# Token rows ahead of context rows in the third mixer, modulation rows kept in a 24-row table, and one PSUM bank per down-product unit in the last two MLPs

## The chip, the cores and the metric

One core of a Trainium2 chip runs the whole program: TensorE (PE), VectorE (DVE), ScalarE (ACT), GpSimd (POOL) and SyncE (SP), each with its own instruction queue. The metric is the device time of one execution in microseconds.

## What is computed

The reference is a chain of two blocks of two layers each on 256 tokens of 1024 columns, all in float32. The first block (two mixers, each followed by a mixture of 32 experts) is not touched by the change. The second block takes its result `x`, a context of 256 rows, and vectors `c`, `c_ctx`:

```
m_l = (silu(c) @ w_mod[i] + b_mod[i]);  m_c = (silu(c_ctx) @ w_mod[i] + b_mod[i])
sh1, sc1, g1, sh2, sc2, g2 = split(m_l, 6)          # csh1, csc1, ... of m_c
hl = modulate(x, norm1_g[i], sh1, sc1)              # rmsnorm * (1 + scale) + shift
i == 0: hc = modulate(ctx, norm1_g[i], csh1, csc1)
        ol = attention_mixer(hl, hc, ...)           # keys and values of ctx and tokens, queries of tokens
i == 1: ol = hyena_mixer(hl, ...)
x = x + g1 * ol
x = x + g2 * (square(relu(modulate(x, norm2_g[i], sh2, sc2) @ w1)) @ w2)
```

The attention mixer projects 1024 columns to a latent query (384 columns, `mla_cq`), a latent key and value (288, `mla_ckv`), 8 query heads (512, `gqa_q`) and 2 key and value heads (256, `gqa_kv`). Both latents are normed and projected again (`mla_q`, `mla_kv`). Eight heads of each kind attend, and `a_out` projects back.

## The kernel before

**Work and buffers.** Weights come in slabs of 128 x 4096 float32 (2 MB) through a ring of six places. SP issues all slab loads in one order, written out by hand (from line 776 on for the part that matters here), and each waits until the last reader of the slab six places back is done (`load`, line 682; `Plan.last_reader`). PSUM has eight banks of 128 x 512; `Plan.take` hands them out in turn, and each filling is a unit with two semaphores, full and drained. Every engine walks its own list of steps. A PE product waits in `claim` until its bank is drained. The plan (`make_plan`, lines 183 to 281), SP, POOL, PE, ACT and DVE all spell the same order.

**Modulation rows.** A row of `m_l` is wanted on all 128 partitions. In one way PE multiplies a slab of `w_mod` with `silu(c)` widened to 128 columns (`c_product`, line 958). In the other DVE forms a partial product over the eight k-tiles (`multiply_c`, line 2061: one tensor_scalar and seven scalar_tensor_tensor of 128 x 512), PE sums it over partitions with a matrix of ones (`sum_up`, line 963), and DVE adds the sum to a bias that POOL loaded as a broadcast row. `pre1` is shift and scale of the first norm (four slabs), `gate1` g1 (two), `pre2` shift and scale of the second norm (four), `gate2` g2 (two).

**Third mixer.** PE goes through the four `mod0.pre1` slabs: a product for the context and a sum for the tokens from each (from line 1303 on). DVE adds all eight to their biases, then norms and modulates first the context, then the tokens (lines 2552 to 2558; `norm_both`, `norm_tile` at line 1969), with ACT's square sums and roots in between (`tile_stats`, line 1537). PE transposes each (`turn`), waits for both, and projects tokens and context together (line 1316). DVE's norms of the latents and heads need a root from ACT; on ACT `root(384, 2)` and `root(256, 4)` stand behind the copies of all four projections (lines 1839, 1840), `root(64, 16)` and `root(64, 8)` behind the copies of the transposed latents. Then come `mla_q`, `mla_kv`, rotations on DVE, transposes of the heads (`mla_qT`, `mla_kT`, PE line 927), and two attentions of 16 steps. After `gqa_o` PE transposes the result (`turn.a_out`) and multiplies with `a_out`; DVE now makes six partial products (`gate1` two, `pre2` four), then runs `modulated_after` (line 2012): gate times result added to h, bias sums, norm.

**The last two MLPs.** Eight steps j of 512 hidden columns. ACT makes a rounded high part of each half slab (`make_high`), DVE the low part (`make_low`, line 2625), both four parts ahead; PE forms each float32 product from three (lines 1398 to 1400 for `w1`, 1411 to 1413 for `w2`). The `w2` half of a step fills four units (two tiles by two halves) in banks 4 to 7, each of 12 matmuls, and DVE adds each to `mlp_y` in SBUF (lines 2653, 2655). At the end `mlp_y` is multiplied by `gate2` and added to h (lines 2666, 2667). The order of one step's halves is MLP_PARTS:

```
MLP_PARTS = [(w, j - w, half) for j in range(MLP_STEPS + 1) for w in range(2) if 0 <= j - w < MLP_STEPS
             for half in range(2)]
```

## Time and profile before

| what | value |
|---|---|
| median of 3 runs | 2659.91 us (2653.01 to 2660.47) |
| profiled execution, its own time | 2655.35 us |
| its span, first to last instruction | 2653.6 us |
| mean granted TensorE clock | 0.939 |
| busy: PE, DVE, ACT | 2370.4, 1965.2, 1342.4 us |
| DMA | 607.80 MB, mean 229 GB/s |

Times in the rows are microseconds from the span's start. The third mixer runs from 1555.8 to about 1855, its MLP to 2047, the fourth mixer to about 2450, the last MLP to 2641. A row's first number is its start or stretch; an idle time in brackets names what ended it. The granted clock is 1.00 at 2.4 GHz and 0.50 at 1.2 GHz. A float32 product of 512 columns leaves two matmul records, a transpose one, an MLP product (rounded parts) one.

### The profile page before, as it was taken

How to read it: one execution, taken by the hardware profiler on the slowest of the kernel's cores; microseconds unless marked ns; L12 is line 12 of the kernel's file. 1: busy time of each engine (PE TensorE's matmuls, PEld its weight loads, DVE VectorE, ACT ScalarE, POOL GpSimd, SP SyncE). 2: the span in 40 equal slices, each digit the busy share in tenths (PEclk: the TensorE clock that was granted, in tenths of full speed). 3: DMA queues.
4: the chain of work that ended last, by engine and by line, in shares of the span. 5: the costliest groups of instructions: out<-in, count | busy, mean ns of one | idle time of the engine just before them, and what ended most of it. 6: DMA issues, size and time to landing. Idle time of an engine off the chain costs nothing.

```text
span 2653.6 us, 29973 instructions
## 1 busy us (share of the span) xinstructions
PE 2370.4 (89%) x11050; PEld 1740.7 (66%) x11050; DVE 1965.2 (74%) x2383; ACT 1342.4 (51%) x1477; POOL 23.9 (1%) x45
## 2 busy tenths in 40 slices
PE   7998999999989879999999987897998668876998
PEld 6557777777764557777777744563887226733887
DVE  3747999999983649999999972558776543468875
ACT  3236888888861428888888821351432011101432
POOL 0000000000000000000000000000000000000000
PEclk9998999999999989999999997898999688988999
DMA  8315989988883217988888872307375401307370
GB/s 323 125 66 202 374 356 373 370 359 359 358 325 104 96 63 317 379 363 361 363 362 362 358 273 81 127 1 258 139 281 183 180 32 64 127 8 272 130 272 16
DMA packets 116505, 607.80 MB, mean 229 GB/s; under 512 B 5300, under 2 KB 8428, under 8 KB 91644
## 3 DMA queue, kind: packets, MB, share of 16 engines
q1 hardware_dynamic: 111536, 588.83, 57.2%
q0 software_dynamic: 4880, 17.76, 1.8%
q8 instruction: 60, 0.98, 0.2%
q14 instruction: 29, 0.24, 0.0%
HBM read 605.51 MB, written 1.05 MB: 229 GB/s over the span
## 4 chain that ended last, share of the span: by engine, by line
PE 54%; DVE 23%; issue 13%; ACT 9%; DVEq 1%; DMA 0%; POOL 0%; SPq 0%; ACTq 0%
PE bank L902 10%; DVE slab_parts L2406 8%; ACT high L1706 5%; PE bank L914 4%; PE bank L1185 4%; PE bank L1137 3%; PE bank L1001 3%; PE bank L1164 2%; PE bank L1398 2%; PE bank L1400 2%; PE bank L1399 2%; PE bank L1126 2%; PE bank L1411 2%; PE bank L1413 2%; PE bank L1412 2%
## 5 line engine op out<-in xcount | busy, mean ns | idle before, releaser
L2406 DVE TENSOR_TENSOR slab_parts<-ring,high 128x2048 fp32r<-128x2048 f32 x384 | 862.3, 2288 | 38.9 <-ACT high L1706 34.4
L1706 ACT ACTIVATE high<-ring 128x2048 fp32r<-128x2048 f32 x384 | 728.5, 1914 | 43.9 <-PE bank L1137 35.6
L1137 PE MATMUL bank<-high,xT_parts 128*128 128x512 f32 x1024 | 294.5, 409 | 18.1 <-DVE slab_parts L2406 14.1
L1137 PE MATMUL bank<-slab_parts,xT_parts 128*128 128x512 f32 x1024 | 278.9, 394 | 0.0
L1549 ACT ACTIVATE arena<-bank 128x512 f32<-128x512 f32 (+4 forms) x162 | 89.4, 586 | 360.8 <-PE bank L902 99.4
L902 PE MATMUL bank<-ring,xT 128*128 128x512 f32 (+3 forms) x576 | 238.3, 575 | 10.2 <-DVE xT L2036 6.2
L1137 PEld LDWEIGHTS bank<-high,xT_parts 128*128 128x128 f32 x1024 | 184.5, 190 | 78.7 <-DVE slab_parts L2406 38.6
L1137 PEld LDWEIGHTS bank<-slab_parts,xT_parts 128*128 128x128 f32 x1024 | 193.9, 189 | 45.5
L1712 ACT ACTIVATE arena<-bank 64x512 f32<-64x512 f32 (+2 forms) x352 | 184.7, 534 | 61.6 <-PE bank L1164 51.5
L902 PEld LDWEIGHTS bank<-ring,xT 128*128 128x128 f32 x576 | 111.3, 194 | 133.9 <-issue 123.3
L1569 ACT ACTIVATE high<-ring 128x2048 fp32r<-128x2048 f32 x64 | 121.8, 1912 | 87.5 <-PE bank L1413 82.2
L2625 DVE TENSOR_TENSOR slab_parts<-ring,high 128x2048 fp32r<-128x2048 f32 x64 | 146.2, 2292 | 20.5 <-ACT high L1569 20.2
L1398 PE MATMUL bank<-xT_parts,high 128*128 128x256 f32 x512 | 148.1, 289 | 10.2 <-DVE slab_parts L2625 10.2
L1164 PE MATMUL bank<-high,hidden_parts 128*128 128x512 f32 x512 | 150.1, 415 | 7.4 <-DVE hidden_parts L2428 4.7
L1400 PE MATMUL bank<-xT_parts,slab_parts 128*128 128x256 f32 x512 | 145.7, 285 | 0.0
L1399 PE MATMUL bank<-xT_low,high 128*128 128x256 f32 x512 | 145.6, 284 | 0.0
L1164 PE MATMUL bank<-slab_parts,hidden_parts 128*128 128x512 f32 x512 | 141.1, 397 | 0.0
L1154 PEld LDWEIGHTS bank<-arena 128*128 128x128 f32 x1024 | 121.8, 192 | 5.9 <-ACT arena L1712 3.1
L1154 PE MATMUL bank<-arena 128*128 128x64 f32 x1024 | 123.0, 273 | 2.2 <-ACT arena L1712 2.2
L887 PE MATMUL bank<-resident,arena 128*128 128x128 f32 x208 | 43.6, 385 | 84.1 <-DVE arena L1981 39.2
L1185 PE MATMUL bank<-arena 128*128 128x512 f32 x256 | 115.3, 592 | 2.7 <-DVE arena L2436 2.7
L1542 ACT ACTIVATE arena<-h 128x1024 f32<-128x1024 f32 x18 | 18.9, 1052 | 192.7 <-DVE stat L1966 192.6
(360 smaller groups left out, 3739.1 us busy)
## 6 DMA issues: line engine op xcount, KB each, us to landing
ring<-in_moe_w_gate SPq DMA_DIRECT2D x64, 2048.0 KB, 8.6
ring<-in_moe_w_up SPq DMA_DIRECT2D x64, 2048.0 KB, 9.1
ring<-in_moe_w_down SPq DMA_DIRECT2D x64, 2048.0 KB, 9.4
ring<-in_mlp_w SPq DMA_DIRECT2D x32, 2048.0 KB, 13.3
ring<-in_w_mod SPq DMA_DIRECT2D x24, 2048.0 KB, 8.0
ring<-in_even_w_in SPq DMA_DIRECT2D x7, 2048.0 KB, 21.4
ring<-in_odd_w_in SPq DMA_DIRECT2D x6, 2048.0 KB, 10.6
ring<-in_h_w_in SPq DMA_DIRECT2D x6, 2048.0 KB, 8.5
```

Of the source, the lines that this page charges most:

```text
L902: last = mm(banks[u.bank][:, 0:n], lhs(k, tile), w[:, k, c0:c0 + n], start=(k == 0), stop=(k == k_tiles - 1))
L1137: last = mm(dst[:, :], seated2[:, 4 * half + k, e], part_[:, k, :], start=(half == a == k == 0), stop=(half == a == 1 and k == 3))
L1154: last = mm(dst[:, (4 * w + f) * SEATS:(4 * w + f + 1) * SEATS], raw[:, w, f * P:(f + 1) * P], fold, start=True, stop=True)
L1164: last = mm(dst[:, :], hidden2[:, f], part_[:, f, :], start=(a == f == 0), stop=(a == 1 and f == 3))
L1185: ins = mm(banks[bank][:, :], weightedT[:, (j // 2) * P:(j // 2 + 1) * P], pair_y[:, (j % 2) * 512:(j % 2 + 1) * 512], start=first, stop=last)
L1398: mm(dst, w_high[:, k, fs], xT_high[:, k, :], start=(k == 0), stop=False)
L1399: mm(dst, w_high[:, k, fs], xT_low[:, k, :], start=False, stop=False)
L1400: last = mm(dst, w_low[:, k, fs], xT_high[:, k, :], start=False, stop=(k == KD - 1))
L1706: act_fn(hi, weight_half(layer, name, half), ACT.Copy).then_inc(sem(f"high{layer}"), 1)
L1712: act_fn(dst, src(banks[u.bank]), func).then_inc(done or moe_drained[layer][u.bank], 1)
L2406: v.tensor_tensor(low, w, hi.bitcast(F32), ALU.subtract).then_inc(sem(f"low{layer}"), 1)
L2625: v.tensor_tensor(w_low, loaded, w_high.bitcast(F32), ALU.subtract).then_inc(sem("mlp_low"), 1)
```

## The change

- **Order of tokens and context.** In `mod0.pre1` the sums of the tokens' last slab come ahead of the context's last product. All four tile_ready calls come at the start, so ACT does both square sums at once. The tokens are normed and transposed first, PE runs `mla_cq` (tokens only) and then transposes the context; statistics of the context get columns of their own.
- **Roots.** Each root stands on ACT right behind the copies of the projection that it norms.
- **Early modulation rows.** DVE makes the partial products of `gate1` and of the shift half of `pre2` before the attention, writing each over the first k-tile of its own slab. `collect` sums two of them on PE into two rows of a 24 x 512 unit (stationary operand: a column of ones among 24), and `keep` adds the unit to `mod_rows`, a 24 x 512 table of all biases, one DMA, in a part of `routers` that is free by then. After `gqa_o` four `spread` products copy one row each to 128 partitions, and ACT copies them to `gate` and `shift`. The scale half of `pre2` goes the old way. SP loads `gate1` ahead of `mla_q` and `pre2` ahead of `a_out`; POOL no longer loads two of the broadcast bias rows.
- **Down products.** Both MLPs keep the four units of the `w2` products open in banks 4 to 7 over all eight steps; DVE's adds and `mlp_y` go. The slabs of steps 0 to 6 are released by a new counter, `mlp_out_used`. In the last step PE waits for half 1's parts, then finishes both halves of tile 0, then of tile 1, and DVE multiplies by `gate2` straight out of PSUM.

The plan's `take` and slab calls follow the new order; the diff leaves them out, with the new columns of the statistics.

```diff
+def mlp_out_used(layer, j, half):
+
+    return 2 * (MLP_STEPS - 1) * layer + 2 * j + half + 1
+
...
+    def collect(self, name, slabs):
+
+        self.take(name)
+        for slab, i in slabs:
+            self.last_reader[self.slabs[slab][i]] = self.units[name][-1]
...
-            if j > 0:
-                self.take(name + ".out", 4, (4, 5, 6, 7))
+            if j == MLP_STEPS:
+                self.take(name + ".out", 4, OUT_BANKS)
                 self.slab(name + ".w2", self.units[name + ".out"][-1])
+            elif j > 0:
+                self.slab(name + ".w2", ("mlp_out_used", mlp_out_used(int(name[-1]), j - 1, 1)))
...
+        def mlp_part_used(eng, layer, n):
 
             w, j, half = MLP_PARTS[n]
-            return U[f"mlp{layer}.hidden"][2 * j + half] if w == 0 else U[f"mlp{layer}.out"][4 * j + 2 * half + 1]
+            if w == 0:
+                full(eng, U[f"mlp{layer}.hidden"][2 * j + half])
+            elif j < MLP_STEPS - 1:
+                eng.wait_ge(sem("mlp_out_used"), mlp_out_used(layer, j, half))
...
-                    sp.wait_ge(bank_full[reader.bank], reader.before + 1)
+                    if isinstance(reader, tuple):
+                        sp.wait_ge(sem(reader[0]), reader[1])
+                    else:
+                        sp.wait_ge(bank_full[reader.bank], reader.before + 1)
...
-            for name in ("gqa_q", "gqa_kv", "mla_q", "mla_kv", "mod0.gate1",
-                         "a_out", "mod0.pre2"):
+            for name in ("gqa_q", "gqa_kv", "mod0.gate1", "mla_q", "mla_kv", "mod0.pre2", "a_out"):
                 stream(name)
...
+            load("mod_rows_loaded", mod_rows, A["b_mod"].rearrange("l (r n) -> (l r) n", n=512))
...
             pool.wait_ge(sem("gqa_o"), 16)
-            load("bias0_gate1", gate, A["b_mod"][0, 2 * D:3 * D].partition_broadcast(P))
-            load("bias0_pre2", shift, A["b_mod"][0, 3 * D:4 * D].partition_broadcast(P))
             load("bias0_pre2", scale, A["b_mod"][0, 4 * D:5 * D].partition_broadcast(P))
...
+            def collect(u, slabs):
+
+                claim(u)
+                for a, (name, i) in enumerate(slabs):
+                    pe.wait_ge(sem(name + ".partial"), i + 1)
+                    n = MOD_ROW[name] + i
+                    last = mm(banks[u.bank][0:MOD_ROWS, :], one_hot[:, MOD_ROWS - 1 - n:2 * MOD_ROWS - 1 - n],
+                              view_k(slab_ap(K[name][i]), KD, 512)[:, 0], start=(a == 0), stop=(a == len(slabs) - 1))
+                tell(last, u)
+
+            def spread(u, name, i, kept):
+
+                n = MOD_ROW[name] + i
+                drained(pe, kept)
+                claim(u)
+                tell(mm(banks[u.bank][:, :], ident[0:MOD_ROWS, n:n + 1].to_broadcast([MOD_ROWS, P]), mod_rows,
+                        start=True, stop=True), u)
...
+            for name, i in PRE1_SUMS:
+                if name == "of_c":
+                    sum_up(U[name][i], "mod0.pre1", i)
+                else:
+                    c_product(U[name][i], K["mod0.pre1"][i], 1)
+            turn("turn.n1_0", u3, 4)
             turned("turn.n1_0")
+
...
+            slab_in(K["mla_cq"][0])
+            project(U["mla_cq"], K["mla_cq"][0], 384, tokens)
+            turn("turn.ctx", ctx_u.rearrange("p (t d) -> p t d", t=NT), 5)
             turned("turn.ctx")
...
-            for name, n in (("mla_cq", 384), ("mla_ckv", 288), ("gqa_q", 512), ("gqa_kv", 256)):
+            for name, n in (("mla_ckv", 288), ("gqa_q", 512), ("gqa_kv", 256)):
                 slab_in(K[name][0])
                 project(U[name], K[name][0], n, all_tokens)
+            pe.wait_ge(sem("one_hot_ready"), 1)
+            collect(U["mods0"][0], MODS0[0])
...
+            collect(U["mods0"][1], MODS0[1])
...
             pe.wait_ge(sem("gqa_o"), 16)
+            for k in range(2):
+                spread(U["mod0.gate1"][k], "mod0.gate1", k, U["mods0"][1])
+            for k in range(2):
+                spread(U["mod0.pre2"][k], "mod0.pre2", k, U["mods0"][1])
             turn("turn.a_out", b2_o)
...
-                if i == 0:
-                    for k in range(2):
-                        sum_up(U["mod0.gate1"][k], "mod0.gate1", k)
-            for k in range(4):
+            for k in range(2, 4):
                 sum_up(U["mod0.pre2"][k], "mod0.pre2", k)
+
+            def out_part(layer, j, half, tile, w_high, w_low):
+
+                u = U[f"mlp{layer}.out"][2 * half + tile]
+                if j == 0:
+                    claim(u)
+                dst = banks[u.bank][:, :]
+                for f in range(4):
+                    h_high, h_low = (mlp_hidden[j % 2][:, a, f, tile * P:(tile + 1) * P] for a in range(2))
+                    mm(dst, h_high, w_high[:, f, :], start=(j == f == 0), stop=False)
+                    mm(dst, h_high, w_low[:, f, :], start=False, stop=False)
+                    last = mm(dst, h_low, w_high[:, f, :], start=False, stop=(j == MLP_STEPS - 1 and f == 3))
+                return last
...
+                    if j < MLP_STEPS - 1:
+                        for tile in range(NT):
+                            last = out_part(layer, j, half, tile, w_high, w_low)
+                        last.then_inc(sem("mlp_out_used"), 1)
+                    elif half == 1:
+                        of_half = [mlp_part(layer, n - 1)[2:], (w_low, w_high)]
+                        for tile in range(NT):
+                            for half in range(2):
+                                w_low, w_high = of_half[half]
+                                tell(out_part(layer, j, half, tile, w_high, w_low),
+                                     U[f"mlp{layer}.out"][2 * half + tile])
...
-            tile_stats(ctx_x, ctx_u)
-            turn("turn.n1_0", ctxT)
             tile_stats(h, u_buf)
-            turn("turn.ctx", xT3)
+            act.wait_ge(sem("ctx_loaded"), 16)
+            tile_stats(ctx_x, ctx_u, NT)
+            turn("turn.n1_0", xT3)
...
+            turn("turn.ctx", ctxT)
+            root(384, 2)
             for j, u in enumerate(U["mla_ckv"]):
...
+            root(256, 4)
...
+            root(64, 16)
...
-            root(384, 2)
-            root(256, 4)
+            root(64, 8)
             for t, u in enumerate(U["turn.cq"]):
...
-            root(64, 16)
-            root(64, 8)
...
+            copies("mod0.gate1", gate)
+            copies("mod0.pre2", shift, units=2)
             turn("turn.a_out", xT3)
...
-                add_bias(bias, [shift, scale], bias.replace("mod", "bias").replace(".", "_"), 2)
+                if name == "a_out":
+                    dma_done(dve, "bias0_pre2")
+                    for u, cs in zip(U[bias][2:4], (slice(0, 512), slice(512, 1024))):
+                        full(dve, u)
+                        drain(v.tensor_tensor(scale[:, cs], scale[:, cs], banks[u.bank][:, :], ALU.add), u)
+                else:
+                    add_bias(bias, [shift, scale], bias.replace("mod", "bias").replace(".", "_"), 2)
...
+            def keep(u):
+
+                full(dve, u)
+                drain(v.tensor_tensor(mod_rows, mod_rows, banks[u.bank][0:MOD_ROWS, :], ALU.add), u)
+
+            def multiply_c(name, i, buffer=None, tiles=(0, KD)):
...
-                w, dst = view_k(slab_ap(idx), KD, 512), partial[name][buffer]
+                w = view_k(slab_ap(idx), KD, 512)
+                dst = w[:, 0] if buffer is None else partial[name][buffer]
...
+            called = [tile_ready() for _ in range(2 * NT)]
+            link(v.memset(one_hot, 0.0))
+            tell(v.memset(one_hot[:, MOD_ROWS - 1:MOD_ROWS], 1.0), "one_hot_ready")
             dve.wait_ge(sem("c_silu"), 1)
             widen_c()
             for i in range(4):
                 multiply_c("mod0.pre1", i, i)
...
+            for i in range(3):
+                add_sum("of_ctx", i)
+            for i in range(4):
+                add_sum("of_c", i)
+            g = gain_row()
+            link(v.scalar_tensor_tensor(scale, scale, 1.0, g, ALU.add, ALU.mult))
+            for t in range(NT):
+                norm_tile(t, called[t], h, u_buf, scale, shift)
+            turn("turn.n1_0", xT3)
+            add_sum("of_ctx", 3)
             dma_done(dve, "ctx_loaded")
-            g = gain_row()
             link(v.scalar_tensor_tensor(scale_c, scale_c, 1.0, g, ALU.add, ALU.mult))
-            norm_both(ctx_x, ctx_u, scale_c, shift_c)
-            link(v.scalar_tensor_tensor(scale, scale, 1.0, g, ALU.add, ALU.mult))
-            norm_both(h, u_buf, scale, shift)
+            for t in range(NT):
+                norm_tile(t, called[NT + t], ctx_x, ctx_u, scale_c, shift_c, first=NT)
             used(g)
-            turn("turn.n1_0", ctxT)
-            turn("turn.ctx", xT3)
+            turn("turn.ctx", ctxT)
+            multiply_c("mod0.gate1", 0)
             for u in U["mla_cq"]:
                 drained(dve, u)
             link(group_norm(z_cq, 2, 384, at(0, 768), row("mla_q_a")))
+            multiply_c("mod0.gate1", 1)
...
+            dma_done(dve, "mod_rows_loaded")
+            keep(U["mods0"][0])
...
+            multiply_c("mod0.pre2", 0)
...
+            multiply_c("mod0.pre2", 1)
+            keep(U["mods0"][1])
             full_attend("mla", b2_o)
             tell(v.tensor_copy(stat[:, 165:166], z_gq[:, 0:1]), "gqa_qk")
             full_attend("gqa", b2_o[:, :, 512:1024])
             turn("turn.a_out", xT3)
-            for i in range(2):
-                multiply_c("mod0.gate1", i, i)
-            for i in range(2):
-                multiply_c("mod0.pre2", i, i)
-            add_bias("mod0.gate1", [gate], "bias0_gate1", 1)
             for i in range(2, 4):
                 multiply_c("mod0.pre2", i, i)
...
-                    else:
-                        for tile in range(NT):
-                            u = U[name + ".out"][4 * j + 2 * half + tile]
-                            full(dve, u)
-                            dst = mlp_y[:, tile, half * 512:(half + 1) * 512]
-                            if j == 0:
-                                drain(v.tensor_copy(dst, banks[u.bank][:, :]), u)
-                            else:
-                                drain(v.tensor_tensor(dst, dst, banks[u.bank][:, :], ALU.add), u)
...
-                    link(v.tensor_tensor(mlp_y[:, t], mlp_y[:, t], gate2, ALU.mult))
-                    link(v.tensor_tensor(h3[:, t], h3[:, t], mlp_y[:, t], ALU.add))
+                    for half in range(2):
+                        u, hs = U[name + ".out"][2 * half + t], slice(half * 512, (half + 1) * 512)
+                        full(dve, u)
+                        drain(v.tensor_tensor(squares[half], banks[u.bank][:, :], gate2[:, hs], ALU.mult), u)
+                        link(v.tensor_tensor(h3[:, t, hs], h3[:, t, hs], squares[half], ALU.add))
```

## Rows read from the trace of the kernel before

**Rows 1.** The page's part 4, shares of the chain that ended last, by engine

```profile
PE 54%; DVE 23%; issue 13%; ACT 9%; DVEq 1%; DMA 0%; POOL 0%; SPq 0%; ACTq 0%
```

**Rows 2.** Windows by stage: busy PE, PEld, DVE, ACT, POOL; clock; DMA share; GB/s

```profile
1555.80:1593.00 37.20, 33.76 (x72) 14.55 (x72) 28.60 (x40) 0.22 (x1) 3.97 (x6) 0.91 0.61 216
1593.00:1617.50 24.50, 7.87 (x32) 6.30 (x33) 17.83 (x26) 9.11 (x17) 0.54 (x1) 0.55 0.15 47
1630.50:1674.00 43.50, 43.12 (x161) 30.10 (x159) 2.06 (x3) 5.98 (x19) 0.00 (x0) 1.00 0.42 145
1674.00:1686.80 12.80, 3.25 (x14) 2.85 (x14) 10.33 (x15) 3.09 (x8) 0.00 (x0) 0.62 0.49 164
1712.20:1719.00 6.80, 5.45 (x48) 5.20 (x48) 0.00 (x0) 6.05 (x13) 0.00 (x0) 1.00 0.80 298
1831.80:1839.60 7.80, 1.90 (x5) 0.57 (x3) 7.42 (x11) 0.00 (x0) 0.00 (x0) 0.87 1.05 388
1862.30:2046.00 183.70, 183.67 (x1153) 165.52 (x1154) 131.19 (x128) 64.37 (x46) 0.00 (x0) 0.98 0.54 194
```

**Rows 3.** The chain of waits from 1555 to 1720, in order of time

```profile
1569.81 6.87 PE bank L902 x16
...
1592.12 0.87 PE bank L967 x2
...
1611.12 0.17 DVE stat L1973
...
1612.64 1.24 DVE arena L1981
...
1617.50 56.13 PE bank L902 x192
```

**Rows 4.** DVE's timeline, third mixer

```profile
1557.69 0.49 DVE L2069 TENSOR_SCALAR arena<-ring,small 128x512 f32<-128x512 f32 x1
...
1563.72 0.49 DVE L2069 TENSOR_SCALAR arena<-ring,small 128x512 f32<-128x512 f32 x1
...
1693.18 0.42 DVE L2089 TENSOR_TENSOR arena<-arena 128x256 f32<-128x256 f32 x1
...
1711.50 0.69 DVE L2605 COPY arena<-arena 128x1024 f32<-128x1024 f32 x1 [0.98 <-ACT arena L1857]
...
1855.26 0.15 DVE L1991 COPY stat<-gain 128x1 f32<-128x1 f32 x1
```

**Rows 5.** ACT's timeline, the copy of mla_cq's second unit

```profile
1630.59 0.49 ACT L1549 ACTIVATE arena<-bank 128x384 f32<-128x384 f32 x1 [4.67 <-PE bank L902]
```

**Rows 6.** PE's timeline, third mixer

```profile
1686.88 3.54 PE L902 MATMUL bank<-ring,arena 128*128 128x384 f32 x5 [1.02 <-ACT arena L1549]
...
1712.25 5.45 PE L927 MATMUL bank<-resident,arena 128*96 128x128 f32 x48 [1.72 <-DVE arena L2605]
1719.12 2.81 PE L938 MATMUL bank<-arena,xT 96*128 96x512 f32 x6 [1.43 <-ACT arena L1549]
...
1799.60 1.97 PE L887 MATMUL bank<-resident,arena 128*128 128x128 f32 x16 [0.76 <-DVE stat L2188]
1802.56 0.67 PE L902 MATMUL bank<-ring,xT 128*128 128x512 f32 x1 [0.99 <-ACT xT L1549]
```

**Rows 7.** The chain of waits at the end of both MLPs

```profile
2046.70 0.25 PE bank L1413
...
2053.11 1.24 DVE arena L2058
...
2054.39 16.49 PE bank L902 x32
...
2641.10 0.25 PE bank L1413
...
2649.23 1.28 DVE arena L1978
```

**Rows 8.** DMA issues from 1799 to 1900: KB each, median us from issue to landing

```profile
ring<-in_mlp_w SPq DMA_DIRECT2D x7, 2048.0 KB, 14.5
```

85 lines of the change are left out of this document (42 added, 43 removed).

## The prediction

> **What bounds the kernel now.** The page's shares of the chain that ended last come first: PE 54%, DVE 23%, issue 13% [rows 1]. No engine bounds the whole, so the stages decide, and I cut the windows view by stage [rows 2]. In the mod0.pre1 stretch PE is busy 33.76 of 37.20 us. In the 24.50 us after it PE works 7.87, at a granted clock of 0.55: norms and transposes of context, then of tokens, one after the other. The four input projections fill PE (43.12 of 43.50). Then 12.80 us with 3.25 of PE: the two latent norms. In the mlp PE is busy 183.67 of 183.70.
>
> The chain of waits [rows 3] shows the products of one 512-column unit (x16) as 6.87 us, a modulated norm tile ending in the row of 1612.64, and the projections starting at 1617.50. The DVE timeline [rows 4] gives one partial product over a slab (6.03 us from 1557.69 to 1563.72), the rotations from 1693.18, mla_qk at 1711.50, the last modulated norm ending at 1855.26. The ACT and PE timelines [rows 5, 6] fix the starts on PE.
>
> **The change, part by part.** I replay the three engines' orders from 1555.8 on with these durations. Clock times of the changed kernel are marked *.
>
> *Start to ckv.* DVE issues four tile_ready and two small memsets before it widens c: about 0.55 us (small copies take 0.15 [rows 4], 0.07 apart). PE's start hangs on issue, not on this; a delay up to 0.55 is in the range. PE's work up to the last of the eight sums is the same: it ends at 1593.0*, but the last unit is now context scale half 1, which only ctx needs. DVE has the four token sums added by 1587.9*, scale is ready at 1589.2* (1.26), and each norm tile costs 2.78 (1611.12 to 1613.90 [rows 3]): 1592.0* and 1594.7*. The square roots of tokens and ctx come out of ACT long before, which removes two waits. PE turns tile 0 from 1593.0* and tile 1 by 1595.75*, the first cq product starts 1.0 after the last transpose, as after turn.a_out (1799.60 + 1.97, then 1802.56 [rows 6]): 1596.75*. One unit of cq is 0.49 + 4.67 = 5.16 at full clock [rows 5], two are 10.3: 1607.1*. ctx is normed by 1603.5* on DVE beside cq; its 16 transposes take 2.0, copies 1.0: ckv starts at 1610.1*, against 1630.4 before (end of cq). **20.2 us.**
>
> *ckv to mla_q.* From ckv to the end of gqa_kv is PE alone, 43.3 us [rows 2]: 1653.5*. On DVE beside it now stand two partial products (12.1) and all of cq's, ckv's and gqa_q's norms, since the roots stand right behind their copies on ACT. ACT's ckv copies queue behind the cq root until DVE is past the first product (1618*), which costs PE nothing, as the banks it asks for next are long drained. lora_ready falls at 1632.6*, long before PE asks. PE then has collect (two products of 512 columns, 0.9 each: 1.8), and 4.0 for the turns of cq and ckv, whose copies on ACT sit behind the root of gk (1656.4*): mla_q starts at 1659.3* against 1686.88 [rows 6]. Gain **27.6** so far: 7.4 more.
>
> *mla_q to the logits.* Here DVE decides. gk's norm ends 1658.1*, keep 0.75, rotations and q part 17.3 (1693.18 to 1710.5 [rows 4]), product pre2[0] 6.03, the k_rope copy 0.7 once mla_kv is drained (1681.7*): mla_qk at 1683.05* against 1712.2. The fourth product ends at 1689.1*; PE's 48 transposes (5.45 [rows 6]) are through at 1688.6*, and the second collect costs about 0.9 more than the copies would: logits at 1690.95* against 1719.12 [rows 6]. Gain **28.2**. SP meets none of this late: gate1 is issued at 1585* and 1593* in place of mla_q and mla_kv, which follow at 1607* and 1626* and are used from 1659* and 1673*; pre2 and a_out all go before 1691*. The two attentions are untouched.
>
> *After attention.* Four spreads stand on PE between gqa_o and turn.a_out. No row has their form (24 weight rows, one column read 128 times), nor the collects' (24 weight columns); the nearest is a sum over ones with as many streamed columns, 0.87 [rows 3]. At half clock that doubles, 1.7, the upper end; below 0.87 I see no way, as 512 columns stream through either way. I take 0.87, **minus 3.5**; their ACT copies keep pace. Gain 24.7 at the first a_out product. Then PE needs 27.6 for a_out with no sum between; DVE does two products (12.1) instead of six beside it and is ready 16 us before a_out ends. Left on the path after the last unit: multiply and add 1.5, two sums of bias 1.5, scale 1.26, two norm tiles 5.55. From a_out's start to the last norm that makes 37.5 against 52.7 before (1802.56 to 1855.26 [rows 4, 6]): **15.2 more, so 40.0 in all** (rounded). POOL loses two broadcast loads here and gains one of 24 rows earlier; mod_rows has some 90 us to land.
>
> *The mlps.* PE has no idle time in them, so 56 of 64 PSUM adds taken off DVE are worth nothing in the steady state; their cover is PE's own work. The tail pays. Before, PE's end at 2046.95 is followed by an add, four passes of 1024 columns and a copy until 2053.11 [rows 7]: 6.2. After it, tile 0 is done while PE works on tile 1, and one multiply, one add (0.7 each) and two small copies remain: 1.8. **4.4 for mlp0.** In mlp1 the end is 2650.5 for PE's 2641.35 [rows 7]: 9.2; after it 1.5, then ACT's square and root 1.7 and a norm pass 1.5, so 4.9: **4.3.** PE in the last step waits for half 1's low part before half 0, but parts are made four ahead. Holding one bank open over all steps is the one thing no row shows; 11 of 12 products of a unit already accumulate at 0.23 each [rows 7], so I take zero. Bounds: zero and, were each of the 768 w2 products as late as a slow-clock one (0.46), 177 us. I stay at the near row.
>
> **Sum:** 40.0 + 4.4 + 4.3 = 48.7 us. Against the profiled execution's own 2655.35: 2606.7. The median shown is 4.6 higher (2659.91 would give 2611.2); I name the middle, **2609**. About 0.3%, 8 us, is what measurement can tell from no change.
>
> **Rivals.**
> 1. *The clock falls in the token turn.* Between the last c product and cq there are only transposes and gaps of about 1 us. Rows with such gaps show full clock: 1.00 in the stretch of the 48 transposes [rows 2], though PE waited 1.72 ahead of them and 1.43 behind [rows 6]. The stretch of 1593 to 1617, with idle times up to 8.6, shows 0.55. If the clock falls, cq's first unit takes 7.9 (from 1617.50 to one unit of 5.16 before 1630.59 [rows 3, 5]) for 5.2, a tile's transposes 1 us more, and mla_q's start after the turns of cq and ckv some 2. About 6 less gained: 2615. The Trainium skill, "TensorE: Matmul & The Clock Gate", section "Part 4: PE-mode transpose", says that full clock does not engage for transposes; by that rule it comes out so, and the 1.00 over 48 transposes speaks against it.
> 2. *DVE becomes the bound between ctx and the logits.* If the early products aren't hidden (four of 6.03), the gain shrinks by 24: 2633. For it: they stand ahead of norms that PE waits for. Against: DVE was busy 2.06 of 43.50 in the projections [rows 2].
> 3. *PE speeds up behind mlp0.* The gap before mod1.pre1's products shrinks from 7.5 to 3.0, and its 16.49 for x32 [rows 7] could be 13.7 (two of 6.87 [rows 3]) at full clock: 2606.
> 4. *Slower: the mlp starves on slabs.* w2 slabs are now released by a counter after both tiles, and w2[0], gate2[0], w1[2], w2[1] are issued together 15 us before the mlp (19 before). If every slab showed its median landing of 14.5 [rows 8] with nothing prefetched, 18 slabs would take 261 for 184.6, in both mlps 153 more: 2762. It decides from (184.6 + 48.7/2)/18 = 11.6 us a slab on. Against: at 388 GB/s [rows 2] a slab takes 5.4, and the counter fires when the bank did.
> That the early rows save nothing, since DVE's multiplies weren't on the path, is excluded: the stretch of 7.80 us has DVE at 7.42 and PE at 1.90 [rows 2].
>
> **Chances.** Forecast 0.70, rival 1 0.14, rival 2 0.07, rival 3 0.05, rival 4 0.02, the rest 0.02 for no change. Forecast's own bounds: starts and small waits give or take 6, own time against median give or take 2. The range takes in rivals 1 and 3: 2594 to 2624. Faster 0.96, same 0.02, slower 0.02.
>
> **What the profile would show.** Right: cq's first product near 1597 (1617.5 before); ckv near 1610; mla_q near 1659 with PE clock 1.00 over the two turns; logits near 1691; four spreads of about 0.9 before turn.a_out; the mlp at 1822; DVE idle at each step's w2 half; 1.8 us from PE's end to widen_c. Wrong: PE waiting on mod0.gate1 or mod0.pre2 partials for over 2 us, a clock of 0.5 in cq, 24-row products dearer than 0.9, ACT in the mlp waiting for DMA and PE with it.

## The result, and the profile after

Over four runs each the changed kernel took 2616.04 us (2612.09 to 2626.35) and the kernel before 2658.7 (2653.01 to 2660.47): a ratio of 0.9849, 95% interval 0.9817 to 0.9881. The medians lie 42.7 us apart; the ratio, which is that of the means, stands for some 40 us. The profiled execution after took 2615.44 us, its span 2613.7, its mean granted clock 0.948 (before 2655.35, 2653.6 and 0.939). Forecast were 2609 us and 48.7 us less, and 2606.7 for the profiled execution.

I read the two traces from one common point, DVE's copy of c that opens the third mixer: 1555.83 us before, 1561.20 after. The changed kernel's profile was thus 5.4 us late where nothing in it had changed yet. "Behind c" below means from that point on in the same trace; * marks a forecast moved by those 5.4 us.

The shares of the chain that ended last (the page's part 4) answer to [rows 1]:

```profile
PE 55%; DVE 22%; issue 13%; ACT 9%; DVEq 1%; DMA 0%; POOL 0%; SPq 0%; ACTq 0%
```

They are the same within one point. The windows by stage, columns as in [rows 2], say more:

```profile
1561.20:1597.60 36.40, 33.23 (x71) 14.68 (x72) 33.71 (x52) 7.03 (x14) 4.67 (x7) 0.91 0.74 247
1597.60:1615.60 18.00, 14.94 (x66) 9.61 (x65) 13.30 (x18) 3.37 (x6) 0.54 (x1) 1.00 0.45 144
1615.60:1658.80 43.20, 43.18 (x160) 30.30 (x160) 25.98 (x35) 5.75 (x19) 0.00 (x0) 1.00 0.26 92
1658.80:1663.70 4.90, 3.63 (x19) 1.86 (x19) 3.48 (x7) 2.59 (x7) 0.00 (x0) 1.00 0.75 240
1688.20:1695.30 7.10, 7.10 (x49) 6.70 (x50) 5.71 (x8) 5.57 (x11) 0.00 (x0) 0.76 0.63 245
1777.50:1784.10 6.60, 6.58 (x9) 2.23 (x9) 0.00 (x0) 1.79 (x3) 1.05 (x2) 0.55 0.52 160
1784.10:1788.70 4.60, 3.64 (x17) 3.24 (x16) 2.33 (x4) 1.79 (x3) 0.00 (x0) 0.53 0.00 0
1833.30:2016.00 182.70, 182.67 (x1155) 164.42 (x1156) 114.97 (x104) 65.82 (x49) 0.00 (x0) 0.99 0.59 211
```

The 24.5 us at clock 0.55 in which context and tokens took turns [rows 2] are gone: in the 18.00 us at that place PE is busy 14.94, at clock 1.00, most of it already the first projection, `mla_cq` (10.56 us). DVE, idle beside the input projections before, is busy 25.98 of 43.20. The rows of 1777.50 and 1784.10 are new and bad: TensorE was busy, and ran near half clock. So is the 0.76 at 1688.20, over the 48 transposes of mla_q. The last row is mlp0, PE busy all through as before; DVE has 16 us less work in it.

PE's timeline, as [rows 6] (start, busy, line, operation, idle time before it):

```profile
1600.23 1.09 PE L912 MATMUL bank<-resident,arena 128*128 128x128 f32 x8 [1.09 <-DVE arena L2049]
1602.32 7.98 PE L927 MATMUL bank<-ring,xT 128*128 128x384 f32 x24 [1.00 <-ACT xT L1613]
...
1615.62 8.00 PE L927 MATMUL bank<-ring,xT 128*128 128x288 f32 x32 [0.99 <-ACT arena L1613]
...
1663.71 21.71 PE L927 MATMUL bank<-ring,arena 128*128 128x384 f32 x56 [1.28 <-ACT arena L1613]
...
1688.18 7.11 PE L952 MATMUL bank<-resident,arena 128*96 128x128 f32 x48 [2.76 <-DVE arena L2710]
1695.22 1.90 PE L1000 MATMUL bank<-ring,w_fox_f 128*24 128x512 f32 x4
1697.05 2.84 PE L963 MATMUL bank<-arena,xT 96*128 96x512 f32 x6
...
1777.52 6.61 PE L1009 MATMUL bank<-routers,resident 24*128 24x512 f32 x8 [0.76 <-DVE stat L2271]
1784.06 3.67 PE L912 MATMUL bank<-resident,arena 128*128 128x128 f32 x16
1788.73 1.52 PE L927 MATMUL bank<-ring,xT 128*128 128x512 f32 x3 [1.00 <-ACT xT L1613]
```

cq starts at 1602.32 (1602.1*), ckv at 1615.62 (1615.5*), mla_q at 1663.71 (1664.7*), the logits at 1697.05 (1696.3*). The four spreads (x8, L1009) took 6.61 us for 3.5, and the 16 transposes behind them 3.67 where the same 16 took 1.97 before [rows 6]. The 48 transposes of mla_q took 7.11 us for 5.45 [rows 6]. Windows inside them, where PE did nothing else, show the clock fall and come back:

```profile
1688.20:1689.00 0.80, 0.80 (x8) 0.80 (x9) 0.76 (x2) 0.14 (x1) 0.00 (x0) 1.00 0.96 374
1691.00:1692.00 1.00, 1.00 (x7) 0.93 (x6) 0.93 (x3) 0.74 (x2) 0.00 (x0) 0.50 1.04 406
1693.00:1694.00 1.00, 1.00 (x11) 1.00 (x10) 0.96 (x2) 0.90 (x3) 0.00 (x0) 1.00 0.00 0
```

The chain at the ends of the MLPs, as [rows 7]:

```profile
2016.31 0.25 PE bank L1444
...
2016.66 0.70 DVE arena L2762
...
2018.36 1.24 DVE arena L2135
...
2605.56 0.25 PE bank L1444
...
2609.32 1.28 DVE arena L2046
```

From PE's end to the widening of c it is 2018.36 - 2016.56 = 1.8 us (6.2 before); from PE's end to the last norm 2610.60 - 2605.81 = 4.8 (9.2 before). Both are as forecast.

### The profile page after: what moved, and what is told of

Read it like the earlier page. It is cut to its first block, busy times and chain, and to the rows that moved or that the text cites. A ratio compares the mean times of both kernels' runs of the same rounds, so it can differ in the third digit from the quotient of the medians.

```text
span 2613.7 us, 29867 instructions
## 1 busy us (share of the span) xinstructions
PE 2372.0 (91%) x11058; PEld 1742.4 (67%) x11058; DVE 1923.1 (74%) x2327; ACT 1345.9 (51%) x1481; POOL 23.6 (1%) x44
## 4 chain that ended last, share of the span: by engine, by line
PE 55%; DVE 22%; issue 13%; ACT 9%; DVEq 1%; DMA 0%; POOL 0%; SPq 0%; ACTq 0%
PE bank L927 10%; DVE slab_parts L2489 8%; ACT high L1770 5%; PE bank L939 4%; PE bank L1228 4%; PE bank L1180 3%; PE bank L1044 3%; PE bank L1207 3%; PE bank L1461 2%; PE bank L1463 2%; PE bank L1462 2%; PE bank L1442 2%; PE bank L1444 2%; PE bank L1169 2%; PE bank L1443 2%
## 5 line engine op out<-in xcount | busy, mean ns | idle before, releaser
L2489 DVE TENSOR_TENSOR slab_parts<-ring,high 128x2048 fp32r<-128x2048 f32 x384 | 862.4, 2288 | 39.1 <-ACT high L1770 34.6
L1207 PEld LDWEIGHTS bank<-high,hidden_parts 128*128 128x128 f32 x512 | 88.6, 192 | 43.4 <-DVE slab_parts L2489 22.2
L1776 ACT ACTIVATE xT_parts<-bank 128x512 fp32r<-128x512 f32 x128 | 76.4, 599 | 78.4 <-PE bank L1169 77.0
```

Source lines behind the costliest of these rows:

```text
L1207: last = mm(dst[:, :], hidden2[:, f], part_[:, f, :], start=(a == f == 0), stop=(a == 1 and f == 3))
L1776: act_fn(dst, src(banks[u.bank]), func).then_inc(done or moe_drained[layer][u.bank], 1)
L2489: v.tensor_tensor(low, w, hi.bitcast(F32), ALU.subtract).then_inc(sem(f"low{layer}"), 1)
```

## Experiments

The experiments' runs lay on three chips. Each median and ratio stands beside runs of the kernel before on the same chip, in which that one took 2657.4 to 2659.5 us. The profiles were also cut at four instructions that every kernel has: the copy of c, the first product of mlp0, the widening of c behind mlp0 (widen_c, with which the fourth mixer begins), and the last hidden product of mlp1. In us:

| kernel | copy of c at | to mlp0 | mlp0 and tail | fourth mixer and mlp1 | rest to the end |
|---|---|---|---|---|---|
| before | 1555.8 | 306.5 | 190.8 | 565.2 | 35.3 |
| before_again | 1554.2 | 304.2 | 190.8 | 565.0 | 35.3 |
| four_banks | 1560.2 | 306.6 | 186.5 | 569.6 | 30.9 |
| four_banks_again | 1561.6 | 306.4 | 186.5 | 569.5 | 31.0 |
| late_rows | 1562.6 | 276.1 | 186.4 | 569.4 | 30.9 |
| changed | 1561.2 | 272.1 | 185.1 | 564.3 | 31.0 |
| changed_again | 1556.0 | 272.0 | 186.5 | 569.6 | 30.9 |
| gap_filled | 1560.4 | 269.2 | 186.5 | 569.5 | 31.0 |
| spread_128 | 1560.6 | 267.4 | 185.7 | 558.7 | 30.9 |
| spread_128_again | 1558.0 | 267.2 | 185.7 | 565.1 | 30.9 |
| turn_first | 1555.5 | 266.5 | 186.0 | 558.9 | 31.0 |
| turn_first_again | 1559.5 | 266.5 | 186.1 | 562.3 | 30.9 |
| both_mixers | 1557.1 | 266.2 | 186.1 | 548.9 | 30.9 |
| warm | 1560.3 | 264.5 | 185.5 | 534.5 | 31.0 |

**The four banks alone** (four_banks): before, with only the MLP hunks of the change.

```diff
-                    for tile in range(NT):
-                        u = U[f"mlp{layer}.out"][4 * j + 2 * half + tile]
-                        claim(u)
...
+                    if j < MLP_STEPS - 1:
+                        for tile in range(NT):
+                            last = out_part(layer, j, half, tile, w_high, w_low)
+                        last.then_inc(sem("mlp_out_used"), 1)
```

> Edit: the kernel before with one part of the change alone, the down products summed over all eight steps in four banks; the third mixer is the old one. Theory A (the terms of the prediction hold one by one): 4.4 us less at the end of the first MLP and 4.3 us less at the end of the last, 8.7 us together: about 2650 against a before of 2658.7. From the end of the first MLP's last product to the widening of c some 1.8 us in place of 6.2. The third mixer takes what it took (first product behind the second mixture of experts to the first MLP: as before within 1 us). Rival B (the two parts work on each other, e.g. the tail of the first MLP is only short because the third mixer's rows came early): under 5 us together. Up to the end of the second mixture of experts this kernel has the instructions of the kernel before: if the 5.4 us that the changed kernel's profile is late there were a side effect of the change, this profile shows the copy of c near 1555.8; if they are variation from run to run, anywhere between 1550 and 1562.

Measured: 2655.62 us (ten runs), ratio 0.9987, interval 0.9973 to 1.0: 3 us less where 8.7 were forecast, and by the interval no change is not ruled out. In the profile both tails are as short as forecast (190.8 to 186.5, 35.3 to 30.9) and the third mixer is unchanged. But the fourth mixer, whose instructions nobody touched, takes 4.4 us longer. So neither theory as I put it: the terms hold one by one, and something else gives half of them back. From mlp0's first product to the start of its last it is 184.3 us (1866.83 to 2051.09), before 184.2: the banks held open cost nothing.

> The kernel before with the four banks alone once more. In its first profile both tails were 4.3 and 4.4 us shorter, as forecast, but the stretch from the widening of c to the last MLP took 4.4 us longer (569.6 against 565.2), and the median over all runs is only 2.7 us lower. Theory A (that stretch depends on where the clock's changes happen to fall; it is the same program text as before): it is 558 to 570 us, no longer than before on average, and the time gained nears 8.7 us with more runs. Rival B (the shorter tail causes it: TensorE idles less there, so the clock falls later, in work): again 569 to 570 and a median within 3.5 us of before.

Measured: 2655.42 us (twelve runs), ratio 0.9983, interval 0.9973 to 0.9993; the stretch took 569.5 again, and the median lies 4.1 us under that of the kernel before (2659.5). The stretch is rival B's, the gain just over its 3.5. The 4.4 us are all lost between the widening of c and the fourth mixer's first input product: 160.8 us before (2053.1 to 2213.9), 165.1 in four_banks (2053.3 to 2218.4). Two rows of PE's timeline, from the filter stage, show how, the kernel before first:

```profile
2119.92 5.84 PE L1453 MATMUL bank<-arena,resident 128*128 128x512 f32 x8 [3.27 <-DVE arena L2709]
2128.30 3.67 PE L1453 MATMUL bank<-arena,resident 128*128 128x512 f32 x8 [2.55 <-DVE arena L2709]
```

and four_banks:

```profile
2120.73 6.05 PE L1479 MATMUL bank<-arena,resident 128*128 128x512 f32 x8 [3.27 <-DVE arena L2729]
2129.32 5.17 PE L1479 MATMUL bank<-arena,resident 128*128 128x512 f32 x8 [2.54 <-DVE arena L2729]
```

The waits are the same; the second eight products took 5.17 us for 3.67, the first 6.05 for 5.84, which makes 1.7 of the 4.4 us. Other products of the stretch differ in the same way. The stage has PE idle up to 13 us at a time and its clock goes up and down, and it is not the waits but the products under half clock that differ.

**The kernel before once more** (before_again, no edit).

> The kernel before once more, for a second profile. Theory A (the fourth mixer's stretch depends on where the clock's changes happen to fall, and the first profile of before was no special case): from the widening of c behind the first MLP to the last MLP 565.2 us within 1, as the 6.2 us of idle time at the tail always let the clock fall there. Rival C (chance alone): 569 us or 560 us. The copy of c lies between 1550 and 1563 us.

Measured: 2659.61 us (ten runs), ratio 1.0004 (0.9991 to 1.0017). The fourth mixer's stretch is 565.0 against 565.2: theory A. The copy of c came at 1554.2.

**The rows taken back out** (late_rows): the changed kernel with gate and shift rows behind attention as before; tokens first, roots behind their copies and four banks stay.

```diff
-            for k in range(2):
-                spread(U["mod0.gate1"][k], "mod0.gate1", k, U["mods0"][1])
-            for k in range(2):
-                spread(U["mod0.pre2"][k], "mod0.pre2", k, U["mods0"][1])
...
+            for i in range(2):
+                multiply_c("mod0.gate1", i, i)
+            for i in range(2):
+                multiply_c("mod0.pre2", i, i)
+            add_bias("mod0.gate1", [gate], "bias0_gate1", 1)
```

> Edit: the changed kernel with the gate and shift rows taken back out of the table: they are multiplied, summed and added behind the second attention as before; tokens ahead of the context, roots behind their copies and the four banks stay. Theory A: against the changed kernel this loses the stretch behind attention (forecast 15.2 us from the a_out turn to the last norm, less the 3.5 us of the spreads, so 11.7 us) and what the half clock took there (4.8 us by the changed kernel's profile, which then is not lost), so it should be only 7 us slower than the changed kernel: about 2623; the first logits of attention come where they came, 135.9 us behind the copy of c, or 0.2 to 1.9 us sooner since the first collect is gone. The clock stays at 1.00 from the last transposes of attention through the a_out turn (1.97 us for 16 transposes). Rival B (the fall of the clock has nothing to do with the spreads and comes at that place by the phase of the earlier work): the a_out turn takes 3 us or more at a clock near 0.50, and the kernel is 11 to 12 us slower than the changed one.

Measured: 2625.36 us (four runs), ratio 0.9879, interval 0.9862 to 0.9896; 9 us above the changed kernel. (SP's order of loads and POOL's bias rows are the old ones too.) Its third mixer gains 306.6 - 276.1 = 30.5 us on four_banks: that is what the order of tokens, context and roots is worth. The early rows are worth 276.1 - 272.1 = 4.0 more as changed, 276.1 - 267.4 = 8.7 where the spreads keep the clock (spread_128), and 9.6 in turn_first, where they also cover a wait. In late_rows' trace the granted clock stays at 1.00 from the logits into the a_out product. That is theory A, with 9 us for 7. Its 48 transposes of mla_q come behind a wait of 1.72 us and take 5.45 us, as before: the longer wait of the changed kernel (2.76 us) comes with the early products.

**What makes the clock fall at the spreads.** Four kernels. First the spreads over 128 rows of the same tile, the other rows times zero (spread_128):

```diff
-                tell(mm(banks[u.bank][:, :], ident[0:MOD_ROWS, n:n + 1].to_broadcast([MOD_ROWS, P]), mod_rows,
+                tell(mm(banks[u.bank][:, :], ident[:, n:n + 1].to_broadcast([P, P]), routers[:, 0:512],
```

> Edit: the changed kernel, but each spread is a product over all 128 rows (the rest of the table's rows times zero) in place of 24. Theory A (products over 24 rows leave most of the array idle, and that is what lets the clock fall while TensorE is busy): the clock stays at 1.00, the eight passes of the spreads take 3.5 us in place of 6.61, the a_out turn 1.97 in place of 3.67, and the a_out product starts 4.8 us sooner in the profile: 216.7 to 222.7 us behind the copy of c in place of 227.5. Rival B (it is the 0.76 us of idle ahead of them, or the two transfers at that place, not the rows): spreads 6.6 us and the turn 3.6 as before, clock 0.50.

Measured: 2608.69 us (four runs), ratio 0.9823, interval 0.9801 to 0.9845. PE's timeline:

```profile
1776.99 3.70 PE L1009 MATMUL bank<-routers,resident 128*128 128x512 f32 x8 [0.77 <-DVE stat L2271]
1780.52 1.91 PE L912 MATMUL bank<-resident,arena 128*128 128x128 f32 x16
```

and its windows over the spreads and the turn:

```profile
1777.00:1780.70 3.70, 3.70 (x10) 1.74 (x11) 0.00 (x0) 1.79 (x3) 1.05 (x2) 1.00 0.55 163
1780.70:1783.40 2.70, 1.73 (x16) 1.50 (x15) 1.92 (x4) 1.79 (x3) 0.00 (x0) 1.00 0.41 165
```

Same place, same idle time ahead (0.77 us), same transfers and columns, only the rows differ: 3.70 us for 6.61, at 1.00. Theory A's numbers came, so it is the rows; how they let the clock fall no run shows. The same kernel once more:

> spread_128 once more, for a second profile and more times. Theory A (over 128 rows the spreads keep the clock, whatever the execution): spreads 3.7 us, the a_out turn 1.76 to 1.97, clock 1.00, a_out product 222.7 us behind the copy of c within 0.5, median near 2608.7. Rival C (the first profile was lucky): 6.6 and 3.6 us at half clock, median near the changed kernel's 2616. For the fourth mixer: in turn_first and spread_128 the stretch from the widening of c to the last MLP took 558.7 to 562.3 us, in six profiles of kernels whose clock fell somewhere in the first MLP's tail 564.3 to 569.6; if that stretch follows how the third mixer ends, it is under 563 us again, if it is chance it may be anything from 558 to 570.

Measured: 2610.12 us median of six runs, one of them at 2643.56, ratio 0.9842 (0.9801 to 0.9883); spreads 3.70, turn 1.91, clock 1.00 again. Its fourth mixer took 565.1 us where the same kernel's first profile had 558.7.

The changed kernel once more (changed_again, no edit):

> The changed kernel once more, unaltered, for a second profile. Theory A (the fall of the clock at the spreads is a property of 24-row products behind idle time): the spreads take more than 6 us again and the a_out turn over 3. Rival C (it is a chance of where the clock's changes lie in the program): spreads 3.5 to 3.7 us and turn 1.97, as in turn_first. Up to the end of the second mixture of experts the copy of c lies anywhere between 1550 and 1563 and the 5.4 us of the first profile are variation; if they are a side effect of the change it is at 1561 again (against that stands turn_first's 1555.5 with the same instructions).

Measured: 2616.15 us (four runs), ratio 0.985 (0.9831 to 0.9868). Windows over spreads and turn:

```profile
1772.10:1778.80 6.70, 6.69 (x9) 2.33 (x10) 0.00 (x0) 1.79 (x3) 1.05 (x2) 0.54 0.40 157
1778.80:1783.40 4.60, 3.61 (x17) 3.23 (x17) 2.36 (x4) 1.79 (x3) 0.00 (x0) 0.56 0.00 0
```

The fall is there again, and in both profiles it comes early: the clock is 1.00 and 0.96 over the first 0.60 us of the spreads, 0.52 and 0.50 over the next 0.90. The copy of c, though, came at 1556.0, and four_banks, which up to there has the instructions of the kernel before, had it at 1560.2 and 1561.6. So the 5.4 us of the first profile are no side effect of the change.

The transposes ahead of the spreads (turn_first):

```diff
+            turn("turn.a_out", b2_o)
             for k in range(2):
                 spread(U["mod0.gate1"][k], "mod0.gate1", k, U["mods0"][1])
...
-            turn("turn.a_out", b2_o)
```

> Edit: the changed kernel with the transposes of the a_out turn ahead of the four spreads, and ScalarE's copies in the same order: the spreads stand where TensorE waited for the turn's copies. Theory A (24-row products let the clock fall): the turn takes 1.97 us at 1.00, the spreads begin at 1.00, and the fall comes in or behind them, so that the a_out product takes 27.6 us plus up to 5 us; the product ends no more than 2 us sooner than in the changed kernel. Rival B (the fall belongs to the idle time ahead of this place, whatever comes behind it): the turn takes 3.6 us at 0.50 and the spreads too are slow, but the wait of 0.98 us behind the turn is covered: the product starts 1 us sooner. Rival C (a chance of the phase): turn and spreads both at 1.00, product starts 5.8 us sooner and takes 27.6.

Measured: 2603.38 us (four runs), ratio 0.9802, interval 0.9779 to 0.9825:

```profile
1771.92 1.97 PE L912 MATMUL bank<-resident,arena 128*128 128x128 f32 x16 [0.76 <-DVE stat L2271]
1773.82 3.69 PE L1009 MATMUL bank<-routers,resident 24*128 24x512 f32 x8
1777.44 2.84 PE L927 MATMUL bank<-ring,xT 128*128 128x512 f32 x6
```

The spreads are over 24 rows, and the clock stayed at 1.00 from the first transpose through the whole product. So neither my theory A (a fall behind them) nor rival B. The numbers are rival C's, but a second profile and spread_128's two speak against chance: with 16 full transposes between the idle time and them, 3.6 us of 24-row products cost nothing, and they also cover the wait for the turn's copies. The edit moves two things at once, the transposes ahead and the long a_out product directly behind; which of them matters is not shown.

> turn_first once more, for a second profile. Theory A (with the transposes between the idle time and the 24-row products the clock holds): transposes 1.97 us, spreads 3.6, clock 1.00, product 27.7. Rival C (chance): one of the three is at half clock this time.

Measured: 2605.75 us (four runs), ratio 0.9803 (0.9788 to 0.9817); 1.97, 3.62 and 27.68 us at full clock again. Then the other half of the pair, idle time filled and spreads left (gap_filled):

```diff
+            claim(U["mod0.gate1"][0])
+            keep_running(U["mod0.gate1"][0].bank, 3)
             pe.wait_ge(sem("gqa_o"), 16)
```

> Edit: the changed kernel with three 128x128x128 products into the first spread's bank in the 0.76 us that TensorE waits for attention's last result; spreads over 24 rows, ahead of the turn, as in the change. Theory A (it takes both, idle time and the products over 24 rows right behind it, to let the clock fall there): clock 1.00, spreads 3.5 to 3.7 us and turn 1.97, 5 us less than the changed kernel from attention to the a_out product. Rival B (6.6 us of 24-row work is enough by itself, wherever it stands ahead of the turn): spreads 6.6 us or the turn 3.6 at half clock again.

Measured: 2618.02 us (four runs), ratio 0.985 (0.9829 to 0.9872). Its timeline from the filler products on:

```profile
1776.15 0.89 PE L1106 MATMUL bank<-resident 128*128 128x128 f32 x6
1777.08 3.69 PE L1009 MATMUL bank<-routers,resident 24*128 24x512 f32 x8
1780.70 3.38 PE L912 MATMUL bank<-resident,arena 128*128 128x128 f32 x16
```

The spreads run at full clock, but the turn behind them takes 3.38 us, at 0.60 over the window from 1780.7 to 1785.0 (0.50 from 1781.5 on). The third mixer is 2.9 us shorter (272.1 to 269.2) where 5 were expected, and no gain shows in the median. So the idle time right ahead is not necessary for a fall, against theory A; rival B's second case came out, 3.38 us for its 3.6. Every fall at this place has the 24 rows in it; behind 16 full transposes it stayed off, behind six short records it did not.

**A version that beats both.** both_mixers is turn_first with spreads over 128 rows, and with the fourth mixer's gate rows and first two pre2 slabs multiplied in VectorE's gaps beside the six input products:

```diff
                 tell(v.tensor_copy(stat[:, 165:166], conv[:, 0:1]), "conv_ready")
+                if i in (1, 2):
+                    multiply_c("mod1.gate1", i - 1)
+                if i in (4, 5):
+                    multiply_c("mod1.pre2", i - 4)
+            keep(U["mods1"][0])
```

> Edit: turn_first, with the spreads over 128 rows, and the same treatment for the fourth mixer: mod1's gate slabs and the first two of mod1.pre2 are multiplied in the gaps that VectorE has beside the six input products, collected into the same table, and spread behind the transposes ahead of the last output product. Theory A (rows made early are worth what they were in the third mixer, as the multiplications move under TensorE's own work): VectorE idles 8.6 us in each input slab's round and one multiplication is 6.3 us, so the rounds keep their 14.7 us; from the transposes of the hyena_out turn to the first product of the last MLP 50 us, as in the third mixer of turn_first, in place of 63.6: 13 us less than turn_first's 2603.4, about 2590. Rival B (the input slabs come later, since six more slabs stand between them in the ring, or the multiplications delay the convolutions): the input rounds grow by 2 us or more each, and the gain is under 5 us. Rival C (the last MLP's first slabs are late now that nothing else is): the MLP starts at a wait for a transfer, gain 5 to 10 us.

Measured: 2601.44 us (five runs, 2590.97 to 2606.3), ratio 0.9783, interval 0.9768 to 0.9798. In the profile, taken of the fastest of the five runs, the end of the mixer came out as theory A says: 49.8 us from the turn (2347.60) to the last MLP (2397.36) for 63.9 in turn_first's first profile and 62.7 in its second and in the kernel before; the rounds of the input products keep their 14.7 us, and the stretch of the table is 548.9 for turn_first's 558.9 and 562.3. The median, though, is only 4.3 us below turn_first's in the same set of runs (2605.75), where theory A had 13. Where the other runs lose the rest no profile shows.

warm is both_mixers with products that nothing reads, in TensorE's waits ahead of the mla_q transposes and in the filter stage, of this kind:

```diff
+                    if j == 0:
+                        keep_running(u.bank, 48)
                     pe.wait_ge(sem("filter_sums"), 2 * n + kind + 1)
```

> Edit: both_mixers with products of the identity by itself, written to a bank that is free, in the waits of TensorE ahead of the transposes of mla_q, in the first transposes behind the first MLP, and in the filter stage (9 to 48 of them in a wait, up to 10 us): nothing reads them. Theory A (the half clock of 2030 to 2078, 2088 to 2102 and 2122 to 2157 us in both_mixers' profile is what that stage pays, and it comes from the idle time): the clock stays at or near 1.00, the 16 filter products take 7.1 us in place of 14.0, the norm sums 3.7 in place of 5.6, 5.9 and 5.1, the 32 transform products 13.7 in place of 16.5 and 16.6; together 10 to 18 us less than both_mixers, and the spread of the times narrows as less hangs on where the clock falls. Rival B (products over 17 and 64 rows let it fall all the same): less than 5 us less. Rival C (the filler products outlast the waits and hold TensorE up): the stage is longer.

Measured: 2577.54 us (five runs, 2574.78 to 2582.28), ratio 0.97, interval 0.9683 to 0.9717. Windows over the filter stage, both_mixers first:

```profile
2030.00:2100.00 70.00, 31.96 (x56) 13.65 (x57) 37.83 (x50) 6.39 (x9) 3.90 (x7) 0.57 0.29 110
2100.00:2167.00 67.00, 48.19 (x95) 20.13 (x94) 29.58 (x18) 10.34 (x17) 0.00 (x0) 0.81 0.09 32
```

and warm:

```profile
2031.00:2092.00 61.00, 53.59 (x334) 42.40 (x332) 37.16 (x52) 6.38 (x9) 3.90 (x7) 0.94 0.37 137
2092.00:2153.00 61.00, 57.45 (x233) 33.58 (x234) 31.73 (x19) 10.33 (x17) 0.00 (x0) 1.00 0.10 35
```

The first 16 filter products went from 14.02 us to 7.13, as expected, and the clock from 0.57 and 0.81 to 0.94 and 1.00. The stretch is 14.4 us shorter (548.9 to 534.5), the third mixer 1.7 (its 48 transposes at full clock), the times lie within 7.5 us. Between the profiles it is 16.6 us, inside the 10 to 18 of theory A, between the medians 23.9. This kernel is about 80 us faster than before and 38 faster than the changed one.

## Why the prediction was right, and where it was off

**Right**, step by step, against the touched stretch of the profile:
- *Start to the logits.* Tokens ahead, roots behind their copies: cq, ckv, mla_q and logits each within 1 us of the forecast behind c. late_rows shows the reorder alone at 30.5 us; the forecast for the logits was 28.2, with the collects and one product of VectorE's charged to it.
- *After attention.* From the a_out product's start (1788.73) to the last norm's end (1826.26) it is 37.5 us, exactly the 37.5 forecast.
- *The tails.* 1.8 us and 4.8 us, forecast 1.8 and 4.9.
- *Holding banks open* costs nothing: 184.3 us from mlp0's first product to the start of its last in four_banks, 184.2 before.

**Off.**
- *The spreads*, "I take 0.87, minus 3.5", with "half clock doubles, 1.7" as the upper end. It was the upper end, 6.61 us, and the fall also slowed the transposes behind it, 3.67 for 1.97. Together 4.8 us that the sum lacked: this is the step of the sum that failed, and the prediction's own sign of being wrong, 24-row products dearer than 0.9, showed (6.61 / 4 = 1.65). Its price at full clock was right (3.70 and 3.62 in the variants); what I left out is that the spreads could themselves let the clock fall and that the work behind them would pay too. That it takes the 24 rows spread_128 shows, with two profiles on either side. Rival 1 had the mechanism at the wrong place: in the token turn the clock was 1.00. The rule that rival 1 cited, in the Trainium skill, "TensorE: Matmul & The Clock Gate", section "Part 4: PE-mode transpose", is that full clock does not engage for transposes. This trace disagrees: the token turn's 8 and 8 transposes took 1.04 and 1.09 us at 1.00, and inside the 48 of mla_q, with nothing else on PE, the clock came back from 0.50 to 1.00 (windows above, and in changed_again and turn_first too).
- *The 48 transposes of mla_q*: 5.45 us in the forecast, 7.11 measured at a clock of 0.76. The forecast had the end of PE's wait ahead of them (mla_qk at 1683.05, measured 1688.18 - 5.4 = 1682.8), but not that a wait of 2.76 us in place of 1.72 would cost clock behind it. It is 7.11 in every kernel with that wait, and 5.45 in late_rows, where it is 1.72, and in warm, where it is filled: another 1.7 us.
- Forecast 40.0 us to mlp0's start; measured 34.4. The missing 5.6 are 4.8 + 1.7, less 0.9 gained in small waits. Where the spreads keep the clock, spread_128 has 39.1. That turn_first has just 40.0 is partly luck: it still pays the 1.7, and covers a wait of 1 us that the forecast left in.
- *The fourth mixer*, which the prediction did not touch beyond rival 3. In one profile of the changed kernel it took 0.9 us less than before, in the other 4.4 more. The tails are worth 8.7 us where they stand but only some 3 to 4 in the medians of four_banks. The table is not mere scatter: five profiles of four kernels (four_banks twice, late_rows, changed_again, gap_filled) lie between 569.4 and 569.6, and in all of them the c products behind mlp0 took 16.9 to 17.0 us, at half clock first. In spread_128 and turn_first, two profiles each, those products took 14.00 us behind the same wait of 3.09, and the stretch 558.7 to 565.1. So the length of the wait does not decide by itself; what does is not settled. One kernel alone (spread_128) still spans 6.4 us.
- *The 5.4 us ahead of the touched stretch* are variation: the copy of c lies between 1554.2 and 1562.6 over all kernels, and at 1561.2 and 1556.0 for the changed kernel itself. They went against the forecast in the profile that it was compared with; what of them is in the medians no profile shows.

So 48.7 us forecast, 45.3 found in the profile behind c (1097.8 to 1052.5 us; in changed_again it is 1059.0, so 38.8), and 42.7 between the medians (40 by the ratio). That 45.3 is so near is in part luck: 34.4 + 4.3 for the third mixer and the last tail, 5.7 for mlp0 and its tail where 4.4 were forecast, and 0.9 in the fourth mixer. The last two hold 2.2 us that changed_again does not have (4.3 there, and 4.4 lost in the fourth mixer).

**Rival 2** (DVE becomes the bound, 24 us lost) did not happen: PE waited 2.76 us at mla_qk, 1.04 more than before. **Rival 3** is not borne out for the changed kernel: the gap shrank as it says (3.09 us for 7.46), but the c products behind mlp0 took 15.70 us in one profile and 16.99 in the other, for 16.49 before. Its 14.00 came only in spread_128, turn_first and both_mixers. **Rival 4**: the slabs kept up, as PE's busy time in mlp0 shows.

## What to carry to other kernels

A small product put where TensorE has just waited is not priced by its columns alone: ask what it does to the clock and what stands behind it. If such a product can read all 128 rows at no cost (3.70 us for 3.69 here), do that; standing it between full transposes and a full product served here too. A saving in idle time of TensorE can be given back further on by the clock (8.7 us in the tails, 3 to 4 in the medians), so measure it by medians of many runs beside the profile; and where TensorE's waits are long and known, filling them can be worth more than shortening them.

## What the runs showed that was not expected

- TensorE, busy without a gap, went to half clock some 0.6 us into four products over 24 rows (6.61 and 6.70 us for 3.7), and not with the same products over 128 rows, twice each; 0.76 us of idle time stood ahead in all four.
- Transposes alone brought full clock back: 0.50 at 1691 to 1692, 1.00 at 1693 to 1694, within 48 of them.
- The same 24-row products behind 16 transposes held 1.00, twice; behind 0.89 us of full products they held it (once) but the transposes after them did not (3.38 us for 1.97).
- Untouched work of one kernel took 558.7 and 565.1 us (spread_128), 564.3 and 569.6 (the changed kernel) in two executions, with half-clock stretches at other places; yet five profiles of four kernels agreed within 0.2 us (569.4 to 569.6).
- Products that nothing reads, 454 matmul records of them, took 17 us off the time behind the copy of c (1032.1 to 1015.5 in the profiles) and 24 off the median.
